# Small vectors packed on the host, one transfer per layer, and the masks waited for later

## The chip, the cores and the metric

The kernel runs on one core of a Trainium2 chip. The core has TensorE (PE, matrix products, with its weight loads PEld), VectorE (DVE), ScalarE (ACT), GpSimd (POOL) and SyncE (SP), whose queue issues nearly all transfers between the chip's memory (HBM) and the core's on-chip memory (SBUF). Each engine works through its own list of instructions in order and waits on semaphores for the others. The metric is the device time of one execution in microseconds (us); lower is better.

## The reference, cut to what matters

The model has two layers of one kind and then one block of another, on 512 tokens of width 1024, all in float32. A layer normalises x, multiplies it with one wide matrix and feeds three attention branches (differential, latent, and cross attention to 256 memory tokens), gates and adds them, and ends in a feed-forward part:

```
for l in range(DEPTH):                       # DEPTH = 2
    h = rmsnorm(x, g_mix[l])
    dq, dk, dv, c_q, c_kv_kr, xq, gate_logits = split(h @ w_in[l])
    y_diff = diff_attention(dq, dk, dv, diff_q_gain[l], diff_k_gain[l], diff_lambda[l], diff_out_gain[l], ...)
    y_mla = latent_attention(c_q, c_kv_kr, mla_qa_gain[l], ..., mla_kva_gain[l], ..., mla_q_gain[l], mla_k_gain[l], ...)
    mem_n = rmsnorm(mem, mem_gain[l])
    y_mem = memory_cross_attention(xq, mem_n, w_mem_kv[l], cross_q_gain[l], cross_k_gain[l])
    gates = sigmoid(gate_logits + b_gate[l])
    x = x + (gates[0] * y_diff @ ... + gates[1] * y_mla @ ... + gates[2] * y_mem @ ...) @ w_out[l]
    x = x + square(relu(rmsnorm(x, g_mlp[l]) @ w_mlp1[l])) @ w_mlp2[l]
```

The second block has three other branches, a state-space scan with a convolution ahead of it, a delta-rule scan and a gated recurrence, then gates and a feed-forward part. It too needs many small vectors: step bias, decay and skip of the state-space branch (`ssm_dt_bias`, `ssm_a_log`, `ssm_d`), the convolution's five taps and bias, the mixing vectors `rwkv_mu`, and gains and biases of 512 to 1792 numbers.

## The kernel before, in words

All work is written out by hand. A `Plan` gives each stage a list of plan times; each engine then runs the steps of all stages in the order of these times (`Plan.run`, L209 to L245). One unit of plan time is about one step of a matrix product. Products get the times 0, 1, 2 and so on, other stages are put beside them. SyncE's steps, and with them the transfers, stand in the same order.

Weights flow through a ring of six blocks in SBUF (`Stream`, L268): SyncE loads a block when the product that used it last is done (L351), ScalarE rounds it to a high part (L331), VectorE subtracts to get the low part (L338), and TensorE makes three products for each (L397 to L399 for tokens, L481 to L483 for features).

**A layer's start.** `Layer1` gives each small vector its own columns in the tile `small`. Nine vectors are laid out as columns (vector element `k * 128 + p` in partition p, column k), so that one transfer has as many runs of 4 bytes as the vector has elements. Three are rows, copied to all 128 partitions. They form two `Load` stages, `cols` and `rows` (one transfer per vector, L1442), at plan times 0.6 and 0.7. The `Load` of the memory tokens (`mem`, 1 MB, L1444) follows at 0.8. `mem` is used by the memory's norm (`Norm`, L679): squares on ScalarE (L705), roots on VectorE (L663 to L674), scaling (L711, L724), then transposes on TensorE (L586) and copies with the gain `mem_gain` (L597, L614). In layer 1 this norm stands at plan times 9.5 to 20.5, amid the products `cq` and `ckv`; in layer 0 at 45.5 to 58.5. `Gains` (L1505) scales some vectors at 15 to 18. In layer 0, `positions` (four numbers per partition) is loaded with 512 runs of 4 bytes.

**The second block's start.** `Constants2` (L1844) loads 22 vectors one by one (L1901) and then three mask transfers (L1903 to L1905) at plan time 0.6. At 3.1 TensorE, ScalarE and VectorE each wait for all of them, vectors and masks; VectorE and ScalarE then compute a few constants (L1931 to L1944, L1914, L1915). Around this stands the product `dt` (128x32 results, plan times 0 to 15): four loads of 32 KB, two passes of two token tiles, 24 products of TensorE ahead of 3.1, 24 until plan time 8, then 48 in the second pass. The two passes share two banks, which VectorE empties by adding the step bias (L2204). The second pair of convolution columns, 1 MB of weights, is loaded into the blocks of the first two `dt` loads, when the second of them is used up (plan time 12 on SyncE). Its split stands on VectorE ahead of the second pass's additions, and these ahead of the first convolution product (L481). The masks themselves are first read at plan time 24 or later.

Of the kernel before, what the change touches and what calls it, by code (L numbers as in the profile page):

```python
# [15 lines left out]
P = 128  # L16
# [4 lines left out]
KD = D // P  # L21
NT = S // P
DEPTH = 2
MEM = 256
NM = MEM // P
# [31 lines left out]
AHEAD = 3  # L57

# [1498 lines left out]
class Layer1:  # L1557
# [3 lines left out]
    def __init__(self, c, l, plan, start, x_marks, hT_free, norm_times):  # L1561
# [20 lines left out]
        self.G, self.R, cols, rows = {}, {}, [], []  # L1582
        for name, n in (("mem_gain", KD), ("b_gate", 3 * KD), ("mla_qa_gain", MQ // P),
                        ("mla_kva_gain", MKV // P), ("diff_out_gain", 1), ("mla_q_gain", 1), ("mla_k_gain", 1), ("cross_q_gain", 1),
                        ("cross_k_gain", 1)):
            self.G[name] = take(n)
            src = i[name][l]
            if src.shape[0] < P:
                self.G[name] = self.G[name][0:src.shape[0], :]
                cols.append((self.G[name], src.unsqueeze(1)))  # L1590
            else:
                cols.append((self.G[name], src.rearrange("(k p) -> p k", p=P)))
        for name, n in (("diff_q_gain", DD), ("diff_k_gain", DD), ("diff_lambda", 4 * DD)):
            self.R[name] = take(n)
            src = i[name][l]
            if name == "diff_lambda":
                src = src.rearrange("a d -> (a d)")
            rows.append((self.R[name], src.partition_broadcast(P)))
# [12 lines left out]
        self.mem_load = Load(c, tag("mem"), [(mem, i["mem"][0].rearrange("(t p) d -> p t d", p=P))], start)  # L1611
# [29 lines left out]
        P_.beside(Gains(c, l, self, [*cols_in, *rows_in]), 15, 18)  # L1641
# [15 lines left out]
        mem_norm = Norm(c, tag("mem norm"), mem, lambda t: [("in", tag("mem"))], G["mem_gain"], cols_in, memT, wide(E[4:8], NM), sums(NM), start,  # L1657
# [186 lines left out]
class Constants2(Stage):  # L1844


    def __init__(self, c, start):
# [22 lines left out]
        self.more = small[:, at - 2 * RC - 3 * P:at]  # L1870
        rows = take(2 * SH + 2 * SH + SH)
        self.dt_bias, self.a_log, self.d_skip = rows[:, 0:32], rows[:, 32:64], rows[:, 64:80]
        self.loads, self.v = [], {}
        for dst, name in ((self.dt_bias, "ssm_dt_bias_2"), (self.a_log, "ssm_a_log_2"), (self.d_skip, "ssm_d_2")):
            src = i[name][0]
            if len(src.shape) == 2:
                src = src.rearrange("a d -> (a d)")
            self.loads.append((dst, src.partition_broadcast(P)))
        for name, n in (("ssm_norm_w_2", 8), ("ssm_conv_b_2", 12), ("rwkv_a0_2", 4), ("rwkv_k_k_2", 4),
                        ("rwkv_k_a_2", 4), ("rwkv_r_k_2", 4), ("rwkv_ln_w_2", 4), ("rwkv_ln_b_2", 4),  # L1880
                        ("hgrn_lb_logits_2", 4), ("hgrn_norm_w_2", 4)):
# [1844 lines left out]
```

## Time and profile before

| | us |
|---|---|
| median of three runs | 3745.13 (3744.01 to 3745.99) |
| the profiled execution | 3747.0 |
| its span, first to last instruction | 3745.7 |
| TensorE busy in the span | 3504.2 (94%) |
| VectorE, ScalarE, GpSimd busy | 2077.8 (55%), 1385.9 (37%), 60.6 (2%) |
| TensorE's mean granted clock | 0.968 of full speed |

The times of rows are from the span's start. A row of a timeline gives the start, the duration, the engine, the line of the kernel, the operation and its tiles, and in brackets the idle time ahead of it with what ended it. "SPq" is an issue on SyncE's queue: its duration is that of the issue, not of the transfer. Products overlap, so two rows of TensorE may begin closer together than they last.

### The profile page before, as it was taken

What the parts mean: (1) busy time and instruction counts of PE and PEld (TensorE: products, weight loads), DVE (VectorE), ACT (ScalarE), POOL (GpSimd) and SP (SyncE); (2) the same over time, 40 slices, a digit from 0 to 9 for tenths busy, and PEclk for the clock granted to TensorE, in tenths of its full rate; (3) what the DMA queues carried; (4) which work ended last, traced back from release to release, by engine and by line L of the source; (5) the groups of instructions that cost most, each with busy time, mean ns of one, the idle gap of its engine ahead of it and who ended that gap; (6) DMA issues with size and microseconds to landing.
All of it is one profiled execution on the core that took longest, in us unless ns stands there. A gap on an engine that the chain in (4) does not pass through costs nothing.

```text
span 3745.7 us, 55883 instructions
## 1 busy us (share of the span) xinstructions
PE 3504.2 (94%) x23320; PEld 2900.7 (77%) x23320; DVE 2077.8 (55%) x3882; ACT 1385.9 (37%) x2494; POOL 60.6 (2%) x32
## 2 busy tenths in 40 slices
PE   7999999899999899999999978998999989889999
PEld 6777688788878677788788867776888778768887
DVE  6777644444447677534444447753655578653434
ACT  4456543332334565433333233232322245222322
POOL 0000000000000000000000000000000033000000
PEclk9999999999999999999999979998999999899999
DMA  4221123233333221232223232224110323232322
GB/s 126 83 64 45 51 79 115 73 100 101 97 111 91 71 58 48 74 106 81 90 93 99 92 85 71 87 82 134 33 34 20 107 68 123 91 118 79 102 94 92
DMA packets 257459, 315.36 MB, mean 84 GB/s; under 512 B 40932, under 2 KB 185316, under 8 KB 257208
## 3 DMA queue, kind: packets, MB, share of 16 engines
q1 hardware_dynamic: 256344, 309.55, 26.2%
q8 instruction: 186, 3.05, 0.3%
q10 hardware_dynamic: 864, 2.23, 0.2%
q14 instruction: 65, 0.53, 0.0%
HBM read 288.15 MB, written 23.59 MB: 83 GB/s over the span
## 4 chain that ended last, share of the span: by engine, by line
PE 75%; DVE 14%; ACT 5%; issue 3%; DMA 2%; SPq 1%; POOL 0%; DVEq 0%; ACTq 0%; POOLq 0%
PE banks L481 11%; PE banks L483 11%; PE banks L482 11%; PE banks L397 8%; PE banks L399 8%; PE banks L398 8%; PE banks L2555 5%; DVE weights_r L338 2%; PE banks L2977 1%; ACT weights_high_r L331 1%; PE banks L586 1%; PE banks L783 1%; PE banks L1058 1%; PE banks L1045 1%; ACT probabilities L1194 1%
## 5 line engine op out<-in xcount | busy, mean ns | idle before, releaser
L338 DVE TENSOR_TENSOR weights_r<-weights,weights_high_r 128x1024 fp32r<-128x1024 f32 (+3 forms) x520 | 601.7, 1163 | 578.5 <-ACT weights_high_r L331 576.9
L481 PE MATMUL banks<-h_T_hi,weights_high_r 128*128 128x512 f32 x1840 | 745.1, 405 | 18.0 <-DVE h_T_lo L822 4.8
L483 PE MATMUL banks<-h_T_hi,weights_r 128*128 128x512 f32 x1840 | 722.8, 393 | 0.0
L482 PE MATMUL banks<-h_T_lo,weights_high_r 128*128 128x512 f32 x1840 | 722.8, 393 | 0.0
L331 ACT ACTIVATE weights_high_r<-weights 128x1024 fp32r<-128x1024 f32 (+3 forms) x520 | 511.7, 992 | 433.3 <-DMA weights<-in_w_mlp 227.9
L481 PEld LDWEIGHTS banks<-h_T_hi,weights_high_r 128*128 128x128 f32 x1840 | 349.7, 190 | 107.5 <-issue 31.0
L483 PEld LDWEIGHTS banks<-h_T_hi,weights_r 128*128 128x128 f32 x1840 | 349.0, 190 | 75.3
L482 PEld LDWEIGHTS banks<-h_T_lo,weights_high_r 128*128 128x128 f32 x1840 | 350.1, 190 | 71.8 <-issue 3.1
L397 PE MATMUL banks<-weights_high_r,h_T_hi 128*128 128x512 f32 (+3 forms) x704 | 293.5, 417 | 30.2 <-issue 16.6
L399 PE MATMUL banks<-weights_high_r,h_T_lo 128*128 128x512 f32 (+3 forms) x704 | 268.6, 381 | 0.0
L398 PE MATMUL banks<-weights_r,h_T_hi 128*128 128x512 f32 (+3 forms) x704 | 267.9, 381 | 0.0
L397 PEld LDWEIGHTS banks<-weights_high_r,h_T_hi 128*128 128x128 f32 x704 | 139.3, 198 | 63.2 <-issue 34.1
L397 PE MATMUL banks<-weights_high_r,cellsM_r 128*128 128x512 f32 (+1 forms) x464 | 182.6, 394 | 2.0 <-DVE gate L1271 2.0
L398 PE MATMUL banks<-weights_r,cellsM_r 128*128 128x512 f32 (+1 forms) x464 | 179.0, 386 | 0.0
L556 DVE TENSOR_TENSOR cellsX<-cellsX,banks 128x512 f32<-128x512 f32 x112 | 76.6, 686 | 176.0 <-PE banks L399 175.9
L399 PE MATMUL banks<-weights_high_r,cellsC_r 128*128 128x512 f32 x432 | 169.0, 391 | 0.0
L398 PEld LDWEIGHTS banks<-weights_r,h_T_hi 128*128 128x128 f32 x704 | 139.7, 198 | 23.6 <-issue 3.9
L399 PEld LDWEIGHTS banks<-weights_high_r,h_T_lo 128*128 128x128 f32 x704 | 138.5, 197 | 23.1
L397 PE MATMUL banks<-weights_high_r,cellsE_r 128*128 128x512 f32 x384 | 150.4, 392 | 3.7 <-DVE cellsS L3348 3.7
L398 PE MATMUL banks<-weights_r,cellsE_r 128*128 128x512 f32 x384 | 149.9, 390 | 0.0
L399 PE MATMUL banks<-weights_high_r,cellsB_r 128*128 128x512 f32 x384 | 149.4, 389 | 0.0
L1358 DVE TENSOR_TENSOR gate<-gate,banks 128x512 f32<-128x512 f32 x64 | 44.0, 688 | 139.2 <-ACT gate L1350 139.2
(545 smaller groups left out, 5742.8 us busy)
## 6 DMA issues: line engine op xcount, KB each, us to landing
weights<-in_w_in SPq DMA_DIRECT2D x57, 1024.0 KB, 5.3
weights<-in_w_in SPq DMA_DIRECT2D x68, 512.0 KB, 3.6
weights<-in_w_mlp SPq DMA_DIRECT2D x32, 1024.0 KB, 5.4
weights<-in_w_mlp SPq DMA_DIRECT2D x64, 512.0 KB, 3.7
weights<-in_ffn_w_in SPq DMA_DIRECT2D x22, 1024.0 KB, 5.1
weights<-in_w_out SPq DMA_DIRECT2D x24, 512.0 KB, 3.7
weights<-in_ffn_w_down SPq DMA_DIRECT2D x22, 512.0 KB, 3.4
weights<-in_w_mem_kv SPq DMA_DIRECT2D x16, 512.0 KB, 3.7
```

The lines of the kernel that those rows point to most:

```text
L331: ac.e.activation(self.part(c.w_high_r, u), self.part(c.w_raw, u), ACT.Copy).then_inc(*ac.tell("high", u))
L338: ve.e.tensor_tensor(self.part(c.w_raw_r, u), self.part(c.w_raw, u), self.part(c.w_high_r, u).bitcast(F32), ALU.subtract).then_inc(*ve.tel ...
L397: pe.e.matmul(out, lhsT=hi[k][:, tok], rhs=wh[:, j, :], start=(k == 0), stop=False)
L398: pe.e.matmul(out, lhsT=hi[k][:, tok], rhs=wl[:, j, :], start=False, stop=False)
L399: mm = pe.e.matmul(out, lhsT=lo[k][:, tok], rhs=wh[:, j, :], start=False, stop=last)
L481: pe.e.matmul(bank[:, :], lhsT=wh[:, k, :], rhs=hi[k], start=(k == 0), stop=False)
L482: pe.e.matmul(bank[:, :], lhsT=wh[:, k, :], rhs=lo[k], start=False, stop=False)
L483: mm = pe.e.matmul(bank[:, :], lhsT=wl[:, k, :], rhs=hi[k], start=False, stop=(k == self.chunks - 1))
L556: ve.e.tensor_tensor(dst, dst, got, ALU.add).then_inc(*ve.frees(*key))
L586: mm = pe.e.transpose(bank[0:m, at:at + rows], src, c.ident[0:rows, 0:rows])
L1358: ve.e.tensor_tensor(y, y, got, ALU.mult).then_inc(*ve.frees(*key))
L2555: mm = pe.e.matmul(bank[h, f * RC:(f + 1) * RC], lhsT=lhsT[h, f, :], rhs=right, start=(n == 0), stop=(n == len(terms) - 1))
```

## The change

Vectors and positions are laid out on the host as they lie in SBUF. Each layer loads its twelve vectors with one transfer of 128 rows of 1704 bytes (213 KB), the second block its 22 vectors with one of 128 rows of 912 bytes (114 KB). In the tile `small` the rows now come ahead of the columns. The memory's load moves from plan time 0.8 to 0.7. The masks of the second block come with two transfers in place of three, of the same 960 KB in all, behind the vectors. The engines wait for the vectors at plan time 3.1, and for the masks at 14.

```
+ROWS_1 = (("diff_q_gain", DD), ("diff_k_gain", DD), ("diff_lambda", 4 * DD))
+COLUMNS_1 = (("mem_gain", KD), ("b_gate", 3 * KD), ("mla_qa_gain", MQ // P), ("mla_kva_gain", MKV // P), ("diff_out_gain", 1),
+             ("mla_q_gain", 1), ("mla_k_gain", 1), ("cross_q_gain", 1), ("cross_k_gain", 1))
+ROWS_2 = (("ssm_dt_bias_2", 2 * SH), ("ssm_a_log_2", 2 * SH), ("ssm_d_2", SH))
+COLUMNS_2 = (("ssm_norm_w_2", 8), ("ssm_conv_b_2", 12), ("rwkv_a0_2", 4), ("rwkv_k_k_2", 4), ("rwkv_k_a_2", 4), ("rwkv_r_k_2", 4),
+             ("rwkv_ln_w_2", 4), ("rwkv_ln_b_2", 4), ("hgrn_lb_logits_2", 4), ("hgrn_norm_w_2", 4),
+             ("ssm_conv_w_2", CONV_TAPS * 12), ("rwkv_mu_2", 2 * 14), ("rwkv_w0_2", 2 * 4))
...
@@ Layer1
+        self.G, self.R = {}, {}
+        first = at
+        for name, n in ROWS_1:
+            self.R[name] = take(n)
+        for name, n in COLUMNS_1:
             self.G[name] = take(n)
+        vectors = small[:, first:at]
...
-        self.cols, self.rows = Load(c, tag("cols"), cols, start, True), Load(c, tag("rows"), rows, start, True)
-        cols_in, rows_in = [("in", tag("cols"))], [("in", tag("rows"))]
+        vectors_load = Load(c, tag("vectors"), [(vectors, i["vectors_1"][l])], start)
+        vectors_in = [("in", tag("vectors"))]
...
-        for n, load in enumerate((self.cols, self.rows, self.mem_load)):
-            P_.at(load, (0.6 + n / 10,))
+        P_.at(vectors_load, (0.6,))
+        P_.at(mem_load, (0.7,))
...
-            P_.at(Load(c, "positions", [(c.pos_i[:, :], i["positions"].rearrange("a (t p) -> p (a t)", p=P)),
+            P_.at(Load(c, "positions", [(c.pos_i[:, :], i["positions"]),
...
@@ Constants2
     def sp(self):
         c, sp = self.c, self.c.sp
         sp.wait_all(self.start)
-        for n, (dst, src) in enumerate(self.loads):
-            sp.e.dma_start(dst, src, allow_slow_non_contiguous=True).then_inc(*sp.tell("cols2_in", n, by=16))
-        c.values[("cols2_in",)] = c.values[("cols2_in", len(self.loads) - 1)]
-        sp.e.dma_start(self.masks[:, 0:12 * RC], c.i["masks_64"]).then_inc(*sp.tell("masks_in", 0, by=16))
-        sp.e.dma_start(self.masks[:, 14 * P:], c.i["masks"][:, 14 * P:]).then_inc(*sp.tell("masks_in", 1, by=16))
-        sp.e.dma_start(self.more, c.i["masks_more"]).then_inc(*sp.tell("masks_in", 2, by=16))
+        sp.e.dma_start(self.vectors, c.i["vectors_2"]).then_inc(*sp.tell("vectors2_in", by=16))
+        sp.e.dma_start(self.small_masks, c.i["masks_small"]).then_inc(*sp.tell("masks_in", by=16))
+        sp.e.dma_start(self.masks[:, 0:12 * RC], c.i["masks_64"]).then_inc(*sp.tell("masks64_in", by=16))
...
     def pe(self):
         yield
-        self.wait(self.c.pe)
+        self.c.pe.wait_ge("vectors2_in")
+        yield
+        self.masks_in(self.c.pe)
         yield
...
@@ Block2
-        plan.at(k, (0.6, 3.1))
+        plan.at(k, (0.6, 3.1, 14))
...
+def vectors(inputs, l, rows, columns):
+
+    def column(x):
+        x = x.reshape(-1)
+        n = -(-x.size // P)
+        return np.concatenate([x, np.zeros(n * P - x.size, x.dtype)]).reshape(n, P).T
+    return np.concatenate([*(np.broadcast_to(inputs[name][l].reshape(1, -1), (P, n)) for name, n in rows),
+                           *(column(inputs[name][l]) for name, n in columns)], axis=1)
+
+
+def laid_out(inputs):
+    packed = [name for name, n in (*ROWS_1, *COLUMNS_1, *ROWS_2, *COLUMNS_2)]
+    arrays = {name: a for name, a in inputs.items() if name not in packed}
+    arrays["positions"] = inputs["positions"].reshape(NT, P).T
+    arrays["vectors_1"] = np.stack([vectors(inputs, l, ROWS_1, COLUMNS_1) for l in range(DEPTH)])
+    arrays["vectors_2"] = vectors(inputs, 0, ROWS_2, COLUMNS_2)
+    return arrays
```

ScalarE and VectorE wait in the same two steps as TensorE does; for ScalarE and VectorE the constants are computed in the first of them, as before.

## Rows read from the trace of the kernel before

**Rows 1.** The profile page, busy time of each engine (us, share of the span, instructions)

```profile
PE 3504.2 (94%) x23320; PEld 2900.7 (77%) x23320; DVE 2077.8 (55%) x3882; ACT 1385.9 (37%) x2494; POOL 60.6 (2%) x32
```

**Rows 2.** Timeline of SyncE's queue, second block: start us, us, engine line operation tiles

```profile
2153.99 0.42 SPq L351 DMA_DIRECT2D weights<-in_w_in  x1
2154.45 1.04 SPq L1901 DMA_DIRECT2D small<-in_ssm_dt_bias  x1
...
2158.14 3.08 SPq L1901 DMA_DIRECT2D small<-in_rwkv_a  x1
...
2174.62 0.43 SPq L1905 DMA_DIRECT2D small<-in_masks_more  x1
...
2189.07 92.53 SPq L351 DMA_DIRECT2D weights<-in_w_in  x8
```

**Rows 3.** Timeline of TensorE, second block; in brackets the idle time before

```profile
2157.16 3.55 PE L783 MATMUL banks<-cellsS,cellsA 128*128 128x128 f32 x16 [1.36 <-DVE cellsS L816]
...
2161.68 0.26 PE L398 MATMUL banks<-weights_r,h_T_hi 128*128 128x32 f32 x1
2161.80 0.26 PE L399 MATMUL banks<-weights_high_r,h_T_lo 128*128 128x32 f32 x1
2178.65 0.37 PE L397 MATMUL banks<-weights_high_r,h_T_hi 128*128 128x32 f32 x1 [16.59 <-issue]
...
2188.67 0.37 PE L399 MATMUL banks<-weights_high_r,h_T_lo 128*128 128x32 f32 x1
...
2196.81 0.76 PE L481 MATMUL banks<-h_T_hi,weights_high_r 128*128 128x512 f32 x1 [2.65 <-DVE cellsC L2204]
```

**Rows 4.** Timeline of VectorE, second block

```profile
2162.32 1.23 DVE L338 TENSOR_TENSOR weights_r<-weights,weights_high_r 128x1024 fp32r<-128x1024 f32 x1 [0.25 <-ACT weights_high_r L331]
2178.65 0.16 DVE L1931 TENSOR_TENSOR small<-small 128x4 f32<-128x4 f32 x1 [15.10 <-DMA small<-in_masks_more]
...
2180.30 1.22 DVE L338 TENSOR_TENSOR weights_r<-weights,weights_high_r 128x1024 fp32r<-128x1024 f32 x1 [0.27 <-ACT weights_high_r L331]
...
2182.68 0.19 DVE L2204 TENSOR_TENSOR cellsC<-banks,small 128x32 f32<-128x32 f32 x1 [1.16 <-PE banks L399]
```

**Rows 5.** Timeline of SyncE's queue, start of layer 1

```profile
1090.38 0.83 SPq L1442 DMA_DIRECT2D small<-in_mem_gain  x1
...
1099.42 0.43 SPq L1444 DMA_DIRECT2D cellsE<-in_mem  x1
```

**Rows 6.** Timeline of ScalarE, start of layer 1

```profile
1108.82 1.06 ACT L705 ACTIVATE cellsE<-cellsE 128x1024 f32<-128x1024 f32 x1 [8.51 <-DMA cellsE<-in_mem]
```

**Rows 7.** Transfers of 1088 to 1104 us: count, KB each, us to landing

```profile
cellsE<-in_mem SPq DMA_DIRECT2D x1, 1024.0 KB, 9.3
```

**Rows 8.** Timeline of TensorE, start of layer 1

```profile
1114.12 0.66 PE L586 MATMUL banks<-identity,cellsE 128*128 128x128 f32 x2 [9.13 <-ACT cellsE L711]
...
1120.54 0.38 PE L586 MATMUL banks<-identity,cellsE 128*128 128x128 f32 x2
```

**Rows 9.** Timeline of SyncE's queue, start of layer 0

```profile
23.13 0.43 SPq L1444 DMA_DIRECT2D cellsE<-in_mem  x1
46.93 7.15 SPq L351 DMA_DIRECT2D weights<-in_w_in  x4
```

**Rows 10.** Timeline of VectorE, start of layer 0

```profile
34.81 0.16 DVE L1473 CAST probabilities<-positions_int 128x4 f32<-128x4 int32 x1
```

**Rows 11.** Transfers of 2150 to 2180 us

```profile
weights<-in_w_in SPq DMA_DIRECT2D x1, 1024.0 KB, 5.9
...
small<-in_ssm_dt_bias SPq DMA_DIRECT2D x1, 16.0 KB, 5.6
```

**Rows 12.** Timeline of ScalarE, second block

```profile
2161.24 1.05 ACT L331 ACTIVATE weights_high_r<-weights 128x1024 fp32r<-128x1024 f32 x1
```

**Rows 13.** Windows, second block: stretch, length, busy (count) by engine, PEclk, DMA share, GB/s

```profile
2158.00:2160.00 2.00, 2.00 (x11) 2.00 (x11) 0.67 (x3) 0.60 (x1) 0.00 (x0) 0.50 0.75 248
```

**Rows 14.** The same view, layer 1

```profile
1109.00:1120.00 11.00, 5.88 (x21) 5.72 (x22) 3.96 (x13) 5.58 (x10) 0.00 (x0) 0.53 0.17 49
```

More of the change, by code:

```diff
@@ L1581, in __init__ @@
         self.lam, k_rope = take(4), take(NT, MR)
[L1582 to L1585, printed above, removed]
-            self.G[name] = take(n)
[L1587 to L1598, printed above, removed]
+        self.G, self.R = {}, {}
[3 more added lines that the diff above has]
+        for name, n in COLUMNS_1:
+            self.G[name] = take(n)
+        for name in ("mla_q_gain", "mla_k_gain"):
+            self.G[name] = self.G[name][0:MQK, :]
+        vectors = small[:, first:at]
         G = self.G
@@ L1869, in __init__ @@
         self.upto64 = (take(RC), take(RC))
[L1870 to L1881, printed above, removed]
-            self.v[name] = take(n)
-            self.loads.append((self.v[name], i[name][0].rearrange("(k p) -> p k", p=P)))
-        for name, taps, n in (("ssm_conv_w_2", CONV_TAPS, 12), ("rwkv_mu_2", 2, 14), ("rwkv_w0_2", 2, 4)):
-            t = take(taps * n)
-            for j in range(taps):
-                src = i[name][0, j]
-                if len(src.shape) == 2:
-                    src = src[0]
-                self.loads.append((t[:, j * n:(j + 1) * n], src.rearrange("(k p) -> p k", p=P)))
-            self.v[name] = t
+        self.small_masks = small[:, 14 * P:at]
+        first, self.v = at, {}
+        for name, n in (*ROWS_2, *COLUMNS_2):
+            self.v[name] = take(n)
+        self.vectors = small[:, first:at]
+        self.dt_bias, self.a_log, self.d_skip = (self.v[name] for name, n in ROWS_2)
         self.mu_rest, self.lb, self.lb1, self.e = take(14), take(4), take(4), take(4)
         assert at <= small.shape[-1], at
-    n = 2
+    n = 3
     def sp(self):
@@ L1911, in act @@
         yield
-        self.wait(ac)
+        ac.wait_ge("vectors2_in")
         ac.wait_ge("logits")
@@ L1916, in act, with masks_in @@
         yield
-    def wait(self, lane):
-        lane.wait_ge("cols2_in")
-        lane.wait_ge("masks_in", 2)
+        self.masks_in(ac)
+        yield
+    def masks_in(self, lane):
+        lane.wait_ge("masks_in")
+        lane.wait_ge("masks64_in")
     def pe(self):
         yield
-        self.wait(self.c.pe)
+        self.c.pe.wait_ge("vectors2_in")
+        yield
+        self.masks_in(self.c.pe)
         yield
@@ L1929, in dve @@
         yield
-        self.wait(ve)
+        ve.wait_ge("vectors2_in")
         ve.e.tensor_tensor(e, lg, lg, ALU.subtract).then_inc(*ve.tell("logits"))
@@ L1946, in dve @@
         ve.stamp("constants 2")
+        yield
+        self.masks_in(ve)
         yield
@@ L3705, in shape_constants @@
         "causal": np.where(q[None, :] <= q[:, None], 0.0, NEG).astype(f),
-        "masks": masks.astype(f),
-        "masks_more": more.astype(f),
+        "masks": masks[:, 0:14 * P].astype(f),
+        "masks_small": np.concatenate([masks[:, 14 * P:], more], axis=1).astype(f),
         "masks_64": masks_64.astype(f),
```

12 lines of the change are left out of this document (6 added, 6 removed).

## The prediction

> **What bounds the kernel now.** I read the profile's page first. TensorE is busy for 94% of the span [rows 1], so a change that removes no matrix work can only win where TensorE stands still, and the 6% that are left lie in many places. The change touches three: the starts of layer 0, of layer 1 and of the second block. So I looked next at SyncE's queue there, then at the same moments on TensorE, VectorE and ScalarE, and last at the times from a transfer's issue to its landing.
>
> At the start of the second block SyncE's queue holds 25 issues in a row, 22 small vectors and three masks, from 2154.45 us to 2175.05 us [rows 2]. TensorE stands 16.59 us until 2178.65 us, and VectorE 15.10 us until the same moment, released by the last mask transfer [rows 3, 4]. A first set of 24 small matmuls (128x32) is done before that wait, 72 more come after it, at 0.213 us each (47 steps from 2178.65 to 2188.67 us), where they took 0.12 us ahead of it [rows 3].
>
> At the start of layer 1 ScalarE stands 8.51 us for the 1 MB transfer of the memory tokens, which SyncE issues at 1099.42 us, after twelve small ones that begin at 1090.38 us [rows 5, 6]; it lands 9.3 us after its issue [rows 7]. TensorE stands 9.13 us for what follows from it, until 1114.12 us [rows 8].
>
> Layer 0 has the same twelve transfers, but they cover nothing: the memory tokens' transfer is issued at 23.13 us, and SyncE's next issue comes at 46.93 us [rows 9]. VectorE's first use of the positions, at 34.81 us, follows its earlier work with no gap [rows 10].
>
> **The change part by part.**
>
> *Second block.* 22 vector transfers become one of 114 KB, three mask transfers become two with the same bytes, and TensorE, ScalarE and VectorE wait at plan time 3.1 for the vectors alone. The issues now end at about 2156 us: three in place of 25, of 0.43 to 1.04 us each; one of before took 3.08 us [rows 2]. When do the vectors land? No row has 114 KB in 912-byte runs, so I bound it. The first vector transfer of before, issued at 2154.45 us, landed after 5.6 us, at 2160.05 us; the 1 MB of weights ahead of it, issued at 2153.99 us, landed after 5.9 us, at 2159.9 us [rows 2, 11]. The bytes themselves cost 0.7 us at the pace at which that 1 MB landed in 5.9 us. So the vectors land at about 2160.7 us. TensorE comes to its wait at 2162.1 us and VectorE at 2163.55 us (2162.32 plus 1.23) [rows 3, 4]: both find it met, and the stall goes. If the issue takes 3.08 us, the vectors come about 2 us later and cost 0.6 us; with the cover of 1.4 us gone, each us of lateness costs a us.
>
> What is late next? I follow the program order from 2162.1 us. TensorE does the other 24 matmuls of its first pass, 2.8 us, to 2164.9 us. Its second pass needs the banks that VectorE empties, and VectorE has first its constants and one weight split: the split starts 1.65 us after the first constant and takes 1.22 us, the bank's addition 0.19 us [rows 4]. That is 2163.55 + 1.65 + 1.22 + 0.19 = 2166.6 us, a new stall of 1.7 us. Then come 24 matmuls, at whose end SyncE may reload the block of weights. After these 48 (2188.67 + 0.21 = 2188.88 us) the row has 7.93 us to TensorE's next product at 2196.81 us: issue, landing, ScalarE's and VectorE's parts of the split, and the bank behind them [rows 2, 3]. This tail stays; it hides the last 24 matmuls, as before. So the product starts at 2166.6 + 24 matmuls + 7.93. At 0.115 us each these end at 2169.4 us and the product starts at 2177.3 us: a gain of 19.5 us. At 0.213 us for these 24 it starts at 2179.6 us, a gain of 17.2 us. If all 48 go slowly, 2162.1 + 10.2 + 7.93 = 2180.2 us, 16.6 us. Which? The granted clock fell to 0.50 (1.2 GHz) from 2158 to 2160 us, behind a standstill of TensorE of 1.36 us, and the 0.12 us shortly after show it back at 2.4 GHz [rows 3, 13]; so the new stall of 1.7 us probably costs some 3 us at the lower level, 14 slow matmuls and 10 quick ones, 4.1 us in all. I take 18 us.
>
> The lower bound on this part is a collision. The mask transfers (960 KB) now start within 1 to 2 us behind the weights that landed at 2159.9 us, where they once started 20 us later. If they shared the engines fully, the weights would land by 960/1024 of 5.9 us later, 5.5 us, against a slack of 1.3 us to ScalarE's use at 2161.24 us [rows 12]: 4.2 us lost, a gain of 13.8 us. The row speaks for the other end: the first vector transfer, 0.46 us behind the weights, landed 0.15 us after them, so later transfers stand behind [rows 2, 11].
> The Trainium skill (DMA: Bandwidth & Descriptors, section "Two DMAs through the same engine are not ordered") says that inside one queue of a DMA engine the descriptors start in order but overlap. By that rule, with which the landings agree, the sum keeps its 18; by full sharing it would lose the 4.2.
>
> The masks' own wait comes at plan time 14, on TensorE ahead of the last dt steps. They land before 2166 us (the weights' 2159.9 us plus 5.5 us); the step is not reached before 2169 us. Cost nothing. The two added wait instructions for masks per engine are below what the rows resolve.
>
> *Layer 1.* Twelve issues become one of 213 KB, and the memory's transfer is issued at 1090.8 to 1091.3 us in place of 1099.42 us (0.43 to 0.83 us for the issue ahead of it) [rows 5]. It lands by 1100.6 us even if it takes its 9.3 us again, and at about 1097 us at the pace of the weights. ScalarE is free from 1108.82 - 8.51 = 1100.31 us [rows 6]. So its squares start at 1100.3 to 1100.6 us, not at 1108.82 us: 8.2 to 8.5 us, and the roots on VectorE, the scaling and the transposes on TensorE follow at the same distance. TensorE, idle from 1104.99 us, then goes on at 1105.6 us. What is late next is that same chain, now 0.6 us behind TensorE. A second part: behind the long stall the granted clock is 0.53 from 1109 to 1120 us, and TensorE works without a gap from 1114.12 to 1120.54 us [rows 8, 14]. At 2.4 GHz these 6.4 us of work would be 3.2 us. Between none and 3.2 us I take 1.5, because each pair of transposes there waits on ScalarE's and VectorE's copies as well, which do not get faster. Layer 1 gives 10 us, between 8.2 and 11.7 us. A transfer of 213 KB ahead of the memory's adds 1 us at most to a landing that has room, unless it takes the full 9.3 us.
>
> *Layer 0.* The vectors, the positions laid out, and the memory 10 us sooner: their cover is the 23 us in which SyncE's queue stands empty. Nothing, and nothing lost: the six weight loads are issued ahead of all of it, as before.
>
> *The sum.* 18 + 10 = 28 us. The profiled execution took 3747.0 us (span 3745.7 us and 1.3 us around it); minus 28 us that is 3719.0 us. It stands 1.9 us above the median of 3745.1 us, from which I count: 3717.1 us. Behind both places all engines had stood still together, and SyncE's later issues wait for TensorE, so nothing else holds the old time, and the shift stays to the end. The likeliest case by its bounds: gains of 22.0 to 31.2 us, 3714 to 3723 us.
>
> **The rivals.** *Only the second block wins.* For it: the memory's transfer took 9.3 us where weights of its size took 5.9 us; something delays it. If that is the store of x and the last weights of 1089 us, it may take still longer at its new place, and the copies around it may fill the rest. Against it: an early start of 8 us would have to be lost in full. Time: 3745.1 - 18 = 3727 us.
>
> *The change doesn't do what it says.* The vectors come no sooner than the masks did, because a transfer in runs of 912 bytes or VectorE's constants hold the block's start anyway. For it: no row has such a transfer. Against it: the small ones landed in 5.6 us, and between 2154 and 2175 us SyncE does nothing but issue. Only layer 1 wins: 3735 us; with neither, 3745 us.
>
> *Slower, by the clock.* The standstills may not be the loss that they look like. If, in place of one long one, TensorE now has several short ones, each with a stretch at 1.2 GHz behind it, work is stretched to twice its length. Place: the two starts. Price: half a us per us at the lower level, so it cancels 28 us once some 56 us more of busy time run there, and ends at 3753 us with 72 us. For it: 1.36 us idle did bring the clock down [rows 13]. Against it: it is back within some 3 us of steady work, and there are two such places, not twenty.
>
> **How the numbers follow.** Both parts as worked out: 0.80. Only the second block, or layer 1 with less than half: 0.10, 3727 us. Only layer 1, second block mostly refilled: 0.05, 3735 us. No change: 0.03. Slower by the clock: 0.02. The predicted time is 3717 us. The range of 3712 to 3728 us takes the likeliest case with 2 us beyond its upper gain and the first rival, and leaves out the others with 0.1 and some of the tails. A measurement of this kernel tells 0.2% from no change, 7.5 us. Faster by more than that: 0.95; within it: 0.03; slower: 0.02.
>
> **What would show it.** In the second block TensorE has no gap of 16 us at its first 128x32 matmuls, SyncE issues three transfers there, and the first 128x512 product starts about 18 us closer to the last transposes (2160.7 us) than the 36.1 us of now. VectorE's first constant follows its weight split directly. In layer 1 the memory's transfer is issued within 1 us of the vectors, ScalarE's wait for it is gone, and TensorE's gap ahead of the transposes is about 0.6 us. Layer 0 up to its gains is unchanged within 1 us. Wrong would be: a wait for the packed vectors over 1 us, weights that land after 2161 us on the old scale, or a gap of like size behind the old one.

## The result: 28.6 us faster, and the profile after

The changed kernel takes 3716.97 us (median of 4 runs, 3713.63 to 3722.11), the kernel before 3745.56 us beside it (4 runs, 3744.01 to 3747.32). The ratio is 0.9929, with a 95% interval of 0.9916 to 0.9941. The forecast was 3717.0 us. The profiled execution took 3719.14 us, its span is 3717.8 us, 27.9 us shorter than that of before.

Lines of the engines' code stand 10 higher in the changed kernel: L338 is now L348, L397 is L407, L481 is L491, L2204 is L2194. Its page shows the same matrix work at the same share, and the transfers under 512 bytes are gone from its packet count (40932 before, 9380 now), which by itself moved nothing:

```profile
PE 3498.8 (94%) x23320; PEld 2895.1 (78%) x23320; DVE 2077.2 (56%) x3882; ACT 1385.3 (37%) x2494; POOL 61.0 (2%) x32
DMA packets 225906, 315.35 MB, mean 85 GB/s; under 512 B 9380, under 2 KB 153892, under 8 KB 225656
```

**Layer 0.** The timeline of SyncE's queue: the memory tokens are asked for 11.0 us sooner than in [rows 9], and the queue's next issue has hardly moved. SyncE's first issue of layer 1 came 0.74 us sooner (1089.64 for 1090.38 us). That is no effect of the change that the runs can show: over all kept traces the issue of layer 1's gain in_g_mix comes between 1061.1 and 1067.4 us, and at 1062.2 and 1067.4 us in two executions of the changed kernel itself.

```profile
12.15 0.50 SPq L1454 DMA_DIRECT2D cellsE<-in_mem  x1
46.58 7.04 SPq L361 DMA_DIRECT2D weights<-in_w_in  x4
```

**Layer 1.** First the timeline of SyncE's queue, then those of ScalarE and TensorE (start, duration, engine and line, in brackets the idle time before), and a window of the stretch that [rows 14] show for before.

```profile
1089.64 0.84 SPq L1454 DMA_DIRECT2D small<-in_vectors  x1
1090.51 0.49 SPq L1454 DMA_DIRECT2D cellsE<-in_mem  x1
...
1099.44 1.05 ACT L715 ACTIVATE cellsE<-cellsE 128x1024 f32<-128x1024 f32 x1
...
1104.73 0.41 PE L596 MATMUL banks<-identity,cellsE 128*128 128x128 f32 x2 [0.51 <-ACT cellsE L721]
...
1114.13 0.44 PE L596 MATMUL banks<-identity,cellsE 128*128 128x128 f32 x2 [0.87 <-DVE cellsC_r L624]
...
1104.00:1120.00 16.00, 14.60 (x102) 13.60 (x101) 11.87 (x36) 10.86 (x26) 0.00 (x0) 1.00 0.30 84
```

The memory's transfer goes out 0.87 us behind the vectors instead of 9 us. It landed after 7.0 us, at 1097.5 us, and ScalarE's squares follow its earlier work with no idle time (8.51 us in [rows 6]). TensorE's gap is 0.51 us (9.13 us in [rows 8]), and the clock column, the first of the last three numbers of the window, reads 1.00 where it read 0.53. The last of the eight transpose pairs starts at 1114.13 us; in the kernel before it started at 1125.82 us. That is 11.7 us, or 10.95 without the 0.74 us from layer 0. At the start of the second block 10.4 us of it are left.

This pair of traces shows the gain at the upper end. The layers of before also ran in two of the experiments below, e2 and e4: there the memory lands after 7.8 us and ScalarE waits 6.82 and 6.69 us for it. From SyncE's issue of the layer's gain in_g_mix to that of in_norm_w at its end, the layer takes 1064.9 us in the kernel before, 1062.5 and 1063.2 us in e2 and e4, and 1053.2 to 1055.3 us in the ten traces with the packed vectors. On average the layer gives about 9 us, and a single pair of traces anything from 7 to 12.

**Second block.** SyncE's queue, and the times from issue to landing:

```profile
2143.35 1.04 SPq L1886 DMA_DIRECT2D small<-in_vectors  x1
2144.44 0.56 SPq L1887 DMA_DIRECT2D small<-in_masks_small  x1
2145.04 0.52 SPq L1888 DMA_DIRECT2D small<-in_masks  x1
2160.57 0.38 SPq L361 DMA_DIRECT2D weights<-in_w_in  x1
...
weights<-in_w_in SPq DMA_DIRECT2D x1, 1024.0 KB, 6.0
small<-in_masks_small SPq DMA_DIRECT2D x1, 576.0 KB, 6.1
small<-in_masks SPq DMA_DIRECT2D x1, 384.0 KB, 6.5
small<-in_vectors SPq DMA_DIRECT2D x1, 114.0 KB, 5.8
```

Three issues stand where 25 stood [rows 2]. The vectors land at 2149.2 us, the masks at 2150.5 and 2151.5 us. VectorE and ScalarE then:

```profile
2151.03 1.22 DVE L348 TENSOR_TENSOR weights_r<-weights,weights_high_r 128x1024 fp32r<-128x1024 f32 x1 [0.26 <-ACT weights_high_r L341]
2152.17 0.15 DVE L1919 TENSOR_TENSOR small<-small 128x4 f32<-128x4 f32 x1
...
2153.80 1.22 DVE L348 TENSOR_TENSOR weights_r<-weights,weights_high_r 128x1024 fp32r<-128x1024 f32 x1 [0.27 <-ACT weights_high_r L341]
2154.94 0.28 DVE L2194 TENSOR_TENSOR cellsC<-banks,small 128x32 f32<-128x32 f32 x2
2167.20 1.22 DVE L348 TENSOR_TENSOR weights_r<-weights,weights_high_r 128x1024 fp32r<-128x1024 f32 x1 [11.98 <-ACT weights_high_r L341]
...
2166.01 2.00 ACT L341 ACTIVATE weights_high_r<-weights 128x1024 fp32r<-128x1024 f32 x2 [12.31 <-DMA weights<-in_w_in]
```

The first constant (L1919) follows the weight split with no wait; the 15.10 us of [rows 4] are gone. TensorE:

```profile
2153.17 0.26 PE L407 MATMUL banks<-weights_high_r,h_T_hi 128*128 128x32 f32 x1
2153.28 0.30 PE L408 MATMUL banks<-weights_r,h_T_hi 128*128 128x32 f32 x1
2153.42 0.37 PE L409 MATMUL banks<-weights_high_r,h_T_lo 128*128 128x32 f32 x1
2155.27 0.36 PE L407 MATMUL banks<-weights_high_r,h_T_hi 128*128 128x32 f32 x1 [1.47 <-DVE cellsC L2194]
...
2165.28 0.37 PE L409 MATMUL banks<-weights_high_r,h_T_lo 128*128 128x32 f32 x1
...
2168.67 0.76 PE L491 MATMUL banks<-h_T_hi,weights_high_r 128*128 128x512 f32 x1 [3.01 <-DVE cellsC L2194]
...
2154.00:2168.00 14.00, 10.39 (x48) 10.31 (x48) 2.02 (x4) 1.99 (x2) 0.00 (x0) 0.50 0.31 91
```

The gap of 16.59 us [rows 3] is gone. In its place stands the new stall, 1.47 us, for the same cause as forecast: the banks (buffers of PSUM, in which TensorE leaves its products) that VectorE empties behind its constants. Behind it all 48 matmuls of the second pass start 0.213 us apart, at a granted clock of 0.50 (1.2 GHz). The first convolution product starts at 2168.67 us, 28.1 us sooner than before; 11.1 us of this were there already when SyncE came to the block, so the block's start gives 17.0 us.

### The profile page after: what moved, and what is told of

Same layout as the page of the kernel before. It is cut to its first block, busy times and chain, and to the rows that moved or that the text cites. A ratio compares the mean times of both kernels' runs of the same rounds, so it can differ in the third digit from the quotient of the medians.

```text
span 3717.8 us, 55840 instructions
## 1 busy us (share of the span) xinstructions
PE 3498.8 (94%) x23320; PEld 2895.1 (78%) x23320; DVE 2077.2 (56%) x3882; ACT 1385.3 (37%) x2494; POOL 61.0 (2%) x32
## 2 busy tenths in 40 slices
DMA packets 225906, 315.35 MB, mean 85 GB/s; under 512 B 9380, under 2 KB 153892, under 8 KB 225656
## 4 chain that ended last, share of the span: by engine, by line
PE 75%; DVE 14%; ACT 5%; issue 3%; DMA 2%; POOL 0%; DVEq 0%; SPq 0%; ACTq 0%; POOLq 0%
PE banks L491 11%; PE banks L493 11%; PE banks L492 11%; PE banks L407 8%; PE banks L409 8%; PE banks L408 8%; PE banks L2545 5%; DVE weights_r L348 2%; ACT weights_high_r L341 2%; PE banks L2967 1%; PE banks L596 1%; PE banks L793 1%; PE banks L1068 1%; PE banks L1055 1%; ACT probabilities L1204 1%
## 5 line engine op out<-in xcount | busy, mean ns | idle before, releaser
L348 DVE TENSOR_TENSOR weights_r<-weights,weights_high_r 128x1024 fp32r<-128x1024 f32 (+3 forms) x520 | 601.7, 1163 | 578.9 <-ACT weights_high_r L341 577.6
L491 PE MATMUL banks<-h_T_hi,weights_high_r 128*128 128x512 f32 x1840 | 745.4, 405 | 18.3 <-DVE h_T_lo L832 4.8
L491 PEld LDWEIGHTS banks<-h_T_hi,weights_high_r 128*128 128x128 f32 x1840 | 350.0, 190 | 107.9 <-issue 31.2
L407 PE MATMUL banks<-weights_high_r,h_T_hi 128*128 128x512 f32 (+3 forms) x704 | 291.8, 415 | 15.4 <-DVE weights_r L348 4.7
L407 PE MATMUL banks<-weights_high_r,cellsM_r 128*128 128x512 f32 (+1 forms) x464 | 182.5, 393 | 2.0 <-DVE gate L1281 2.0
L407 PEld LDWEIGHTS banks<-weights_high_r,h_T_hi 128*128 128x128 f32 x704 | 137.6, 196 | 48.9 <-issue 19.0
L407 PE MATMUL banks<-weights_high_r,cellsE_r 128*128 128x512 f32 x384 | 150.4, 392 | 3.7 <-DVE cellsS L3338 3.7
```

What stands on the lines that cost most here:

```text
L348: ve.e.tensor_tensor(self.part(c.w_raw_r, u), self.part(c.w_raw, u), self.part(c.w_high_r, u).bitcast(F32), ALU.subtract).then_inc(*ve.tel ...
L407: pe.e.matmul(out, lhsT=hi[k][:, tok], rhs=wh[:, j, :], start=(k == 0), stop=False)
L491: pe.e.matmul(bank[:, :], lhsT=wh[:, k, :], rhs=hi[k], start=(k == 0), stop=False)
```

## The experiments

All were timed against the kernel before on the same chip; the ratio is worked out from single runs and can differ a little from that of the two medians. The kernel before had medians of 3742.2, 3744.2, 3745.0 and 3744.7 us in the four sessions (17, 9, 11 and 7 runs), single runs from 3737.8 to 3753.5.

| kernel | median us (range) | ratio to before, 95% |
|---|---|---|
| e1 layers only | 3730.9 (3728.7 to 3736.2) | 0.9972 (0.9960 to 0.9984) |
| e2 second block only | 3724.3 (3720.7 to 3725.4) | 0.9949 (0.9937 to 0.9962) |
| e3 masks waited for early | 3714.1 (3710.1 to 3714.8) | 0.9920 (0.9906 to 0.9933) |
| e4 later wait only | 3737.6 (3734.3 to 3743.2) | 0.9988 (0.9980 to 0.9997) |
| e5 memory first | 3731.9 (3727.4 to 3738.0) | 0.9972 (0.9960 to 0.9983) |
| e6 other banks | 3717.7 (3710.0 to 3719.6, and one of 10463) | 0.9924 (0.9910 to 0.9937) |
| e7 no lookahead | 3712.9 (3710.5 to 3715.6) | 0.9919 (0.9905 to 0.9932) |
| e8 vectors last | 3719.2 (3711.8 to 3720.2) | 0.9931 (0.9918 to 0.9945) |
| e9 four banks | 3700.5 (3699.7 to 3701.8) | 0.9882 (0.9869 to 0.9895) |
| e10 four banks, no lookahead | 3711.1 (3705.7 to 3715.0) | 0.9909 (0.9895 to 0.9923) |
| e11 changed kernel again | 3719.0 (3713.7 to 3725.8) | 0.9931 (0.9917 to 0.9945) |
| e12 four banks again | 3707.4 (3706.3 to 3715.2) | 0.9902 (0.9885 to 0.9919) |

Single runs of one kernel differ by up to 16 us, so a step of 1 to 5 us is read from the traces, on a local scale: the start of the first convolution product (128x512) behind SyncE's issue of the norm's gain, in_norm_w, at the end of layer 1. It is 68.97 us in the kernel before and 51.90 us in the changed one.

**One half of the change at a time.** e1 keeps the packed vectors of the layers and has the second block of before; e2 has the second block of the change and the layers of before.

```
e1: Constants2 of before: 22 vector transfers, 3 of masks, one wait at 3.1
e2: Layer1 of before: 12 vector transfers, then the memory's
```

> Layers 0 and 1 as changed (packed vectors, positions laid out, memory transfer next), the second block as before. My theory (two separate gains, each from SyncE's queue of issues ahead of something waited for) expects 10 to 11 us less than the kernel before, all of it at the start of layer 1: ScalarE's wait of 8.5 us for the memory tokens gone, the transposes of the memory 9.4 us closer to the end of the products before. The rival, that the layers gain nothing lasting because engines downstream hold the old time, expects under 3 us.

> The second block as changed, the layers as before. Two separate gains: 17 to 18 us less than the kernel before; with the run of the layers alone the two add up to the whole within 2 us. The rival, that the gains are not independent (the clock, or a common cause), expects a sum that is off by over 3 us.

e1's ScalarE and TensorE, then e2's ScalarE:

```profile
1102.28 1.05 ACT L715 ACTIVATE cellsE<-cellsE 128x1024 f32<-128x1024 f32 x1
2171.55 0.37 PE L407 MATMUL banks<-weights_high_r,h_T_hi 128*128 128x32 f32 x1 [17.02 <-issue]
```

```profile
1106.91 1.06 ACT L715 ACTIVATE cellsE<-cellsE 128x1024 f32<-128x1024 f32 x1 [6.82 <-DMA cellsE<-in_mem]
```

Each half removes its own stall and leaves the other. By the medians e1 gives 11.3 us and e2 17.9 us, together 29.2 us for the 28.6 of the whole change. By the ratios they give 10.5 and 19.1 us, together 29.6 us for 26.6, and the intervals of the two ratios are each some 9 us wide. So the kernel times allow a sum but don't prove it. The traces do at the two places: layer 1 from in_g_mix to in_norm_w takes 1055.3 us in e1 and 1054.6 us in the changed kernel; the product of the local scale comes at 69.40 us in e1 (68.97 before) and at 51.96 us in e2 (51.90 in the changed kernel). Packing the layers' vectors and packing the block's vectors are independent there, as the sum had assumed.

**What in layer 1 gives the gain?** e5 is the kernel before with one line turned: the memory's transfer ahead of the twelve small ones, nothing packed.

```
-        for n, load in enumerate((self.cols, self.rows, self.mem_load)):
+        for n, load in enumerate((self.mem_load, self.cols, self.rows)):
```

> The kernel before, but in each layer the memory tokens are loaded ahead of the twelve small vectors, which stay twelve transfers. If the gain of layer 1 is the memory's place in SyncE's queue and not the packing, this gives the same 10 to 11 us: the memory is issued at 1090.4 us and lands by 1100 us, the vectors land by 1106 us, ahead of their first use in the gains at about 1109 us. If the many 4-byte runs slow down the memory's transfer wherever they stand (sharing the engines), part of ScalarE's 8.5 us wait stays and the gain is well under 8 us.

Its SyncE queue and ScalarE:

```profile
1091.44 0.83 SPq L1444 DMA_DIRECT2D cellsE<-in_mem  x1
1092.32 0.53 SPq L1442 DMA_DIRECT2D small<-in_mem_gain  x1
...
1093.51 5.01 SPq L1442 DMA_DIRECT2D small<-in_mla_qa_gain  x1
...
1101.46 1.05 ACT L705 ACTIVATE cellsE<-cellsE 128x1024 f32<-128x1024 f32 x1
```

The same ratio as e1, and a layer of 1055.2 us. So the gain in the layer is the memory's place in the queue. Packing is one way to move it forward; another order of the same issues does as well. The small transfers themselves, one of which held the queue for 5.01 us, cost nothing once nobody stands behind them.

**What in the second block gives the gain?** e4 is the kernel before with its 25 transfers, and only the wait for the masks moved to plan time 14. e3 is the changed kernel with the masks waited for at 3.1 again, together with the vectors.

```
e4: -        plan.at(k, (0.6, 3.1))
    +        plan.at(k, (0.6, 3.1, 14))
e3: +        self.masks_in(lane)   # behind each wait for vectors2_in
```

> The kernel before with one part of the change: the wait for the masks moved to plan time 14, all 22 vectors and 3 masks still loaded one by one. If the many issues are the cost, the release comes when the last vector lands, at 2175.3 instead of 2178.65 us on the scale of before: 3.4 us gained, the gap on TensorE 13.2 us instead of 16.6 us. If the masks' wait is what counts, the gain is near the whole 17 us of the second block.

> The changed kernel, but all three engines wait for the masks together with the vectors at plan time 3.1 (the third part of the change undone). In the changed kernel the masks landed at 2150.5 and 2151.5 us, TensorE comes to that wait at 2151.2 us and VectorE at 2152.2 us: so I expect no difference (under 1 us), and the later wait is worth nothing once the vectors are packed. The rival, that the later wait is a working part of the gain, expects 3 us or more lost.

TensorE in e4, then in e3:

```profile
2175.22 0.40 PE L397 MATMUL banks<-weights_high_r,h_T_hi 128*128 128x32 f32 x1 [13.09 <-DMA small<-in_rwkv_w]
```

```profile
2150.75 0.25 PE L407 MATMUL banks<-weights_high_r,h_T_hi 128*128 128x32 f32 x1 [0.81 <-DMA small<-in_masks]
```

With the vectors unpacked, the later wait shortens the stall from 16.6 to 13.1 us and no further, since the last of the 22 small transfers then releases it; the product moves by 3.4 us and the kernel by 4.6. With the vectors packed, the early wait costs a stall of 0.81 us that leaves no trace: the product comes at 51.86 us (51.90), because the second pass waits for VectorE at the same moment either way. Of the 17 us the packing carries all, and the later wait is worth nothing beside it. That packing is needed isn't shown: no run keeps the 22 transfers and issues them sooner, or moves the engines' wait for the vectors itself.

**The vectors' place among the masks.** e8 is the changed kernel with the vectors issued behind the 960 KB of masks.

```
-        sp.e.dma_start(self.vectors, c.i["vectors_2"])...
         sp.e.dma_start(self.small_masks, c.i["masks_small"])...
         sp.e.dma_start(self.masks[:, 0:12 * RC], c.i["masks_64"])...
+        sp.e.dma_start(self.vectors, c.i["vectors_2"])...
```

> The changed kernel with the packed vectors of the second block issued behind the two mask transfers (960 KB) instead of ahead of them. If transfers of one queue land one behind the other, the vectors land at about 2152 us on the scale of the changed kernel, where TensorE comes at 2151.2 us and VectorE at 2152.2 us: 0 to 1 us lost. If they share the engines evenly, the vectors land no later than now or 1 MB of weights lands later; ScalarE's first split (2149.95 us) then moves, by up to 4 us.

```profile
2150.91 0.28 PE L407 MATMUL banks<-weights_high_r,h_T_hi 128*128 128x32 f32 x1 [0.78 <-DMA small<-in_vectors]
```

A stall of 0.78 us in TensorE's first pass, and again none of it at the product (51.90 us). Counted from the issue of the weights, the vectors land 2.6 us later than in the changed kernel (8.9 for 6.3 us), and the weights 0.2 us later (6.2 for 6.0 us), so the case of evenly shared engines didn't come.

**The stall that stayed, and the slow matmuls.** The new stall and the gap of 3.01 us ahead of the first product both end with VectorE's addition L2194, which empties the two banks of the dt projection ("gemm 2"). e7 takes away what VectorE does ahead of the last additions, the splits of the convolution's first weights; e6 gives the projection the four banks of the ring "work", which it shares with the norm.

```
e7: -            far = last + (3 if u < last else 1 + AHEAD)
    +            far = last + (3 if u < last or self.tag == "dt" else 1 + AHEAD)
e6: -  ... DtOut(...), ring="gemm 2", together=2,
    +  ... DtOut(...), ring="work", together=2,
```

> The changed kernel without the split of the next convolution weights ahead of the last two additions of the dt product on VectorE and ScalarE (the look-ahead of that one job cut by one). The tail of 8 us between the 48th matmul and the convolution's first product is then only the end of the dt product itself: the first 128x512 product starts at about 2165.7 instead of 2168.7 us, 3 us gained, if nothing behind it waits for the later split; otherwise none.

> The changed kernel with the dt product in four other PSUM banks (ring work, banks 4 to 7) instead of the two that the convolution products use. This takes away the new stall of 1.5 us of TensorE behind the first pass, and with it, by my theory, the low clock of the second pass (48 matmuls at 0.213 us each where 0.111 us are possible); the convolution's first product no longer waits for VectorE's additions either. Expected: 8 to 11 us less than the changed kernel (about 3707 us), the granted clock at 1.0 through the second pass, first 128x512 product at about 2159 us. If the low clock does not come from the stall, the second pass stays slow and the product starts at about 2164 us: 4 to 5 us gained. If the weights' reload is the bound, the gain is given back at the third convolution product.

TensorE in e7, then in e6:

```profile
2158.25 0.36 PE L407 MATMUL banks<-weights_high_r,h_T_hi 128*128 128x32 f32 x1 [1.47 <-DVE cellsC L2194]
```

```profile
2157.19 0.40 PE L407 MATMUL banks<-weights_high_r,h_T_hi 128*128 128x32 f32 x1 [1.21 <-DVE cellsC L2194]
```

Both close the gap ahead of the product (48.72 and 49.53 us on the local scale, for 51.90), neither the stall ahead of the second pass. e6 failed in its purpose: this ring's turn, shared with the norm's transposes, most likely gives the second pass a bank of the first again, which I read from the code and not from a row. One of e6's five executions took 10463 us, for which no trace was kept, and its cause is open; the ratio leaves it out, and the median of the other four is 3714.7 us. The whole kernel's time doesn't resolve these 2 to 3 us: the ratios of both, 0.9919 and 0.9924, are within the interval of the changed kernel's 0.9929.

e9 gives the projection banks 0 to 3, where at that time nothing else works. e10 adds e7's edit to it. e11 is the changed kernel again, for comparison in the same session.

```
e9: -  ... DtOut(...), ring="gemm 2", together=2,
    +  ... DtOut(...), ring="gemm", together=2,
```

> The changed kernel with the dt projection's four token tiles in four PSUM banks (ring of banks 0 to 3) in place of two, so that its second pass of 48 matmuls waits for no VectorE addition. In the changed kernel this pass starts after a stall of 1.47 us and all its 48 matmuls then take 0.213 us each, where the first pass ran at 0.111. Theory (the stall is what brings the low clock): no stall, the second pass at 0.111, so 1.5 + 48 x 0.10 = 6.4 us sooner at matmul 95 (from 48.5 to some 42.1 us behind the issue of in_norm_w); the first convolution product is then bound by VectorE's and ScalarE's weight split, which is where it waits now (3.0 us), so the end of the block moves by 0 to 3 us. Rival (the clock falls anyway there, whatever the stall, because the 8 us before were idle): the stall's 1.5 us go, the 48 matmuls stay at 0.213, matmul 95 at 47.0. Whole kernel: 3714 to 3717 us by either; the median alone does not separate them, the matmuls' durations do.

> The four banks of the previous kernel, and in the same projection's last pass no weight blocks of the convolution split ahead of VectorE's additions (the lookahead of the kernel with no gap before the first convolution product, which gave 3712.9 us). If what bounds the first convolution product is TensorE alone once the lookahead is gone, it starts 0.2 us behind matmul 95: at 42.3 us if the stall was what brought the low clock (about 9.6 us before the changed kernel's 51.9, so about 3707 us for the kernel), at 47.2 if the clock falls anyway (4.7 us, 3712). Rival: the splits of the convolution's first weight blocks, or their landing, are late then: it waits for them at 45 to 49 us and the gain over the lookahead alone is 0 to 4 us.

> The changed kernel itself, unedited, on the same chip as the two before it, to compare them with: 3717 us, with single executions from 3710 to 3722, 0.992 to 0.994 of the kernel before. If the spread of single executions is the granted clock falling at different places, a second profile of the same kernel shows stretches of the same instructions with another clock: in the window of the second block around 2458 to 2540 us (1.00 and 0.96 in the first one) or behind it.

TensorE in e9, with a window of the first pass and one of the second:

```profile
2145.88 3.39 PE L793 MATMUL banks<-cellsS,cellsA 128*128 128x128 f32 x16 [1.35 <-DVE cellsS L826]
...
2152.98 0.26 PE L407 MATMUL banks<-weights_high_r,h_T_hi 128*128 128x32 f32 x1
2153.09 0.36 PE L408 MATMUL banks<-weights_r,h_T_hi 128*128 128x32 f32 x1
2153.29 0.38 PE L409 MATMUL banks<-weights_high_r,h_T_lo 128*128 128x32 f32 x1
...
2163.53 0.37 PE L409 MATMUL banks<-weights_high_r,h_T_lo 128*128 128x32 f32 x1
2163.74 0.77 PE L491 MATMUL banks<-h_T_hi,weights_high_r 128*128 128x512 f32 x1
...
2150.00:2153.00 3.00, 3.00 (x30) 3.00 (x29) 2.60 (x8) 1.58 (x4) 0.00 (x0) 1.00 0.22 85
2154.00:2160.00 6.00, 6.00 (x30) 6.00 (x29) 1.07 (x3) 0.00 (x0) 0.00 (x0) 0.50 0.02 3
```

The stall is gone, and so is the gap ahead of the product, which comes at 47.16 us. But the clock falls at 2153.09 us all the same, with TensorE busy for the whole 6.00 us of the window and before it, and all that is left of the projection runs 0.213 us apart. My theory that the stall brings the low clock falls; its rival, which named 47.0 us for matmul 95, holds in its numbers (47.0 us measured). The reason that I gave with it, idle time of 8 us before, does not hold: when the clock fell, TensorE had worked without a gap since 2145.88 us, 7.2 us long, and had stood only 1.35 us ahead of that. The changed kernel's own rows say it too, once one looks: its matmul at 2153.42 us, ahead of the stall, already lasts 0.37 us. What TensorE ran before the fall in both is a row without a gap, 16 transposes and then these 128x32 matmuls, 0.11 us apart at a clock of 1.00 for the last 3 us. I have no run that changes their width, so their part in it stays open.

The kernel time of e9 was a surprise: 3700.5 us, 18.5 us under e11, where the local gain is 4.7. e10, with the same local gain (47.11 us), came out at 3711.1. In the profiled executions 4.0 us of the distance between e9 and e11 are there at in_norm_w already, ahead of anything that the edit touches; the rest lies at the edit and behind it. Here is the stretch between the same two stores of kept_z in SyncE's queue, with the same 281 matmuls, as a window (columns as in [rows 13]) of the changed kernel, of e9 and of e12:

```profile
2401.52:2465.43 63.91, 58.20 (x281) 47.19 (x282) 27.83 (x40) 16.24 (x21) 0.00 (x0) 0.89 0.24 74
```

```profile
2396.69:2455.70 59.01, 53.30 (x281) 44.03 (x282) 27.82 (x40) 16.25 (x21) 0.00 (x0) 0.97 0.26 81
```

```profile
2400.10:2462.17 62.07, 56.36 (x281) 45.84 (x282) 27.83 (x40) 16.25 (x21) 0.00 (x0) 0.92 0.25 77
```

Idle time is the same 5.7 us in all three; what differs is TensorE's busy time, and with it the clock column: 0.89, 0.97, 0.92. e12 is e9 unedited, run to see which of this comes back:

> The kernel with four banks for the dt projection once more, unedited, since it came out 18 us under the changed kernel where its own local gain is 4.7 us (1.5 of the stall, 3.2 of the gap ahead of the first convolution product; its second pass ran at the lower clock level with no stall before it). If the other 12 us are the granted clock of the stretches behind it, and these follow from when TensorE gets there, the second profile shows the same stretches: 59.0 and 120.7 us between the first and second store of kept_z and the second store of kept_hgrn_f (63.9 and 124.2 in the changed kernel), and 3698 to 3703 us. If that was luck of one chip session, the stretches are back at 62 to 64 and 124, and the kernel is at 3708 to 3713 us.

It took 3707.4 us (3706.3 to 3715.2; the profiled one is the 3715.2, which took 6 us more behind kept_hgrn_g than e9 and e10 did). The local gain repeats (the block's first store of kept_shift comes 5.8 us sooner than in the changed kernel in both), two later stretches repeat in e9, e10 and e12 (15.84 for 18.82 us ahead of the fourth set of gates, 23.90 for 27.07 us ahead of the second kept_hgrn_g, each at a clock of 1.00 for 0.82 and 0.87), and the kept_z stretch gives 62.02 us in e10 as in e12. Its 59.01 us are e9's alone. So neither of my two cases holds in full.

Are the later stretches a gain of the four banks? The other traces speak against it. From the first convolution product to that second store of kept_hgrn_g the matrix work is the same in all kernels. It takes 788.6 us in e9, 791.9 and 792.3 us in e10 and e12, 800.4 and 799.4 us in the changed kernel and e11. But it also takes 793.5 and 794.3 us in e1 and e5, and 796.7 and 797.1 us in e2 and e4, all with the two banks; and e2 and e4 have the 23.9 us ahead of kept_hgrn_g too, e1 the 15.84 us ahead of the gates. Only the 4.7 us at the edit are shown to be the banks' own. What comes behind depends on something that I can't name, perhaps on when TensorE gets there.

e11 answers its own question as well: the changed kernel's second profile repeats the kept_z stretch (63.83 for 63.91 us, TensorE busy for 58.12 for 58.20 us) and the one behind it, up to the second kept_hgrn_f (123.93 for 124.20 us), so where I had expected a difference there is none. Its span is 3.2 us longer, and it had lost 5.2 us ahead of layer 1's in_g_mix already.

Taken together the four banks give 0.9882, 0.9909 and 0.9902 of the kernel before, against 0.9931 of the changed kernel in the session of the first two. It is the version that beats both: one word of code beyond the change, and 8 to 18 us on top of it as measured (the 8 in e10, with e7's edit), of which 4.7 are explained.

## Why the prediction was right, step by step

- **The second block's stall goes**: held. Vectors forecast at 2160.7 us on the scale of before, measured 2149.2 + 11.1 = 2160.3 us. e2 shows the gain alone, e1 its absence.
- **A new stall of 1.7 us behind VectorE**: held in place and cause, measured 1.47 us. Its end was forecast at 2166.6 us, measured 2155.27 + 11.10 = 2166.4 us.
- **"Some 3 us at the lower level, 14 slow matmuls and 10 quick ones"**: this is the term that was mis-sized. All 24 were slow, 5.1 us in place of 4.1, and the 24 behind them as well. The reason given for it, the stall, is refuted by e9, and so is the remark under the rivals that the clock is back within some 3 us of steady work: in e9 it stayed at 0.50 through 10.4 us of small matmuls without a gap. The cost stood among the bounds (17.2 us for 24 slow matmuls).
- **The tail of 7.93 us**: measured 8.29 us (2155.27 plus 24 x 0.213 is 2160.38 us, to 2168.67). Its last part is the wait behind VectorE's weight split, which e7 and e9 show to be 3 us that could go. The prediction took this tail as given.
- **Sum of the block**: 18 us forecast, 17.0 measured. The weights ahead of the masks landed after 6.0 us, as before (5.9), so the collision that would have cost 4.2 us didn't happen. The vectors, 0.48 us behind the weights in the queue, landed 0.3 us behind them. The rule cited there from the Trainium skill (DMA: Bandwidth & Descriptors, "Two DMAs through the same engine are not ordered"), by which the descriptors of one queue start in order but overlap, fits these landings.
- **The masks' wait at 14 costs nothing**: held; the last mask lands at 2151.5 us. e3 and e4 add that it brings nothing either beside the packing.
- **Layer 1, 8.5 us plus 1.5 of clock**: in this pair of traces ScalarE's squares came 8.6 us sooner net of layer 0 (1108.82 to 1099.44, less 0.74). The second term was short: 2.3 us more at the last transposes, 0.6 us of them lost again by the end of the layer. 10 us forecast, 10.4 measured here and about 9 over all traces, since the kernel before was profiled with a memory transfer of 9.3 us where e2 and e4 show 7.8. The reason fits too: with no long stall the clock stayed at 1.00. The landing was forecast for 1097 us and came at 1097.5 us.
- **Layer 0, nothing**: held; 0.7 us lie within what executions of one kernel differ by there.
- **The rivals**: the packed transfer in 912-byte runs was not slow (5.8 us); the memory was not delayed at its new place (7.0 us for 9.3). The slower case had several stretches at the low clock in place of one; the rows show one of 10 us behind the new stall, where the kernel before had one of 15 us, so there was nothing to cancel the gain.

10.4 us in layer 1, 17.0 us in the block and 0.7 us ahead of both make 28.1 us at the first convolution product; the spans differ by 27.9 us. That they agree so well is partly luck: the same work from there to kept_hgrn_g takes 788.6 to 800.4 us over the kept traces, and 800.1 and 800.4 us in the two that are compared. That the forecast met the median to 0.03 us is luck outright: single runs of either kernel spread over 8 us or more.

## What to carry to other kernels

Look at what stands behind a row of small transfers in the issuing queue: at 0.43 to 0.92 us an issue, with one of 2.8 us among them, twelve of them held a 1 MB transfer back by 9 us, and moving that one forward gave as much as packing. When a long stall goes, follow the program order to the next wait and ask for its buffers too: here two more PSUM banks for one small projection, one word in the code, were worth another 4.7 us where they act. Judge steps of a few us by local distances in the trace, since the whole kernel's time moves by more than that for reasons of the clock.

## What the runs showed of the hardware that I had not expected

The granted clock fell to 1.2 GHz in the middle of an unbroken row of small matmuls (e9, 2153.09 us) and came back 3.1 us after the 128x512 products began (their durations go from 0.63 to 0.40 us by 2166.83 us). In the changed kernel, with 3.01 us idle ahead of the first product, the slow products last 5.2 us, from 2168.67 to 2173.90 us; in e7, with nothing idle there, they last 5.1 us, so the idle time isn't the reason for that length either.

The clock is also one reason why executions of the same kernel differ. Over one stretch of 281 equal matmuls the busy time was 56.36 and 53.30 us in two executions of the kernel with four banks, at equal idle time, and 58.20 and 58.12 us in two of the changed kernel. Behind an edit such stretches can give or take more than the edit itself; which it will be, nothing in these traces let me forecast.
